# A new order in two mixers and a mask added by a matrix product, in a one-core transformer kernel

## The reference, cut to what matters

```python
# hybrid mixer: x_lru, z, xbc, dt come from one projection h @ w_in
y_lru = rg_lru(causal_conv(x_lru)) * gelu(gate)      # a recurrence over time
xbc = silu(causal_conv(xbc)); xs, bm, cm = split(xbc)
y = ssd_chunked(xs, dt, a, bm, cm) + d * xs           # needs cm @ bm^T per group
out = concat(y_lru, rms_norm(y * silu(z))) @ w_out

# matrix-memory mixer (mlstm): 4 heads of width 512
hh = head_layer_norm(mlstm_chunkwise(q, k, v, i, f))
out = ((hh * norm_g + skip * xc) * silu(z)) @ w_down

# attention kind C: 16 query heads of 64, 2 key heads, a window of 128, a sink per head
sc = where(mask, q @ k^T / 8, -inf)
m = max(max(sc), sink);  p = exp(sc - m)
out = (p / (sum(p) + exp(sink - m))) @ v @ w_out
```

## Time and profile before

| | |
|---|---|
| median of 3 runs | 2538.01 us (2534.19 to 2540.05) |
| profiled execution | 2538.91 us, its span 2537.1 us |
| TensorE (PE) busy | 2421.6 us, 95% |
| VectorE (DVE) busy | 1750.9 us, 69% |
| ScalarE (ACT) busy | 1197.2 us, 47% |
| GpSimd (POOL) busy | 99.5 us, 4% |
| mean granted clock of TensorE | 0.983 |
| instructions | 46504 |

### The profile page before, as it was taken

How to read it: one execution, slowest core, us unless ns; L and a number is a source line. 1 busy time by engine, 2 the same in 40 slices (tenths; PEclk the granted TensorE clock), 3 DMA queues, 4 the chain that set the end, 5 groups by cost and what they waited for, 6 DMA issues and landing times.

```text
span 2537.1 us, 46504 instructions
## 1 busy us (share of the span) xinstructions
PE 2421.6 (95%) x19275; PEld 2325.5 (92%) x19275; DVE 1750.9 (69%) x2240; ACT 1197.2 (47%) x1488; POOL 99.5 (4%) x168
## 2 busy tenths in 40 slices
PE   5999899999999998899998999999998899998998
PEld 5999888999999988899987999889997799987998
DVE  7787788777777865555586755777657666686665
ACT  5334854433433654333455434655335543556433
POOL 2110000010010000000000000110000000000000
PEclk8999999999999999999999999999999999999999
DMA  8886455787687432355433555325552255443552
GB/s 314 318 306 242 154 187 208 252 289 271 239 286 277 160 133 79 118 200 184 152 145 117 182 182 182 133 101 182 183 183 97 84 199 198 150 149 117 190 191 100
DMA packets 75417, 471.49 MB, mean 186 GB/s; under 512 B 8616, under 2 KB 9000, under 8 KB 26664
## 3 DMA queue, kind: packets, MB, share of 16 engines
q1 hardware_dynamic: 56288, 400.79, 43.8%
q0 software_dynamic: 18432, 67.12, 7.5%
q10 hardware_dynamic: 584, 2.00, 0.2%
HBM read 468.83 MB, written 1.05 MB: 185 GB/s over the span
## 4 chain that ended last, share of the span: by engine, by line
PE 81%; DVE 9%; ACT 6%; issue 3%; DMA 1%; SPq 0%; ACTq 0%; DVEq 0%
PE bank L2135 23%; PE bank L2137 23%; PE bank L2136 22%; ACT w_hi L615 2%; PE bank L2146 2%; PE bank L2141 2%; DVE w_lo L1243 2%; PE bank L2142 2%; ACT ARENA L891 1%; DVE ARENA L1432 1%; DVE ARENA L1699 1%; DVE ARENA L1696 1%; PE bank L2213 1%; PE bank L2219 1%; DVE XT L1346 1%
## 5 line engine op out<-in xcount | busy, mean ns | idle before, releaser
L1243 DVE TENSOR_TENSOR w_lo<-w_raw,w_hi 128x2048 fp32r<-128x2048 f32 x369 | 845.6, 2293 | 357.2 <-ACT w_hi L615 356.2
L615 ACT ACTIVATE w_hi<-w_raw 128x2048 fp32r<-128x2048 f32 x371 | 707.9, 1911 | 545.7 <-PE bank L2137 535.1
L2135 PE MATMUL bank<-h_hi,w_hi 128*128 128x256 f32 x3376 | 950.4, 282 | 0.7 <-issue 0.3
L2137 PE MATMUL bank<-h_hi,w_lo 128*128 128x256 f32 x3376 | 941.0, 279 | 0.0
L2136 PE MATMUL bank<-h_lo,w_hi 128*128 128x256 f32 x3376 | 939.9, 278 | 0.0
L2135 PEld LDWEIGHTS bank<-h_hi,w_hi 128*128 128x128 f32 x3376 | 633.3, 188 | 8.4 <-issue 7.8
L2136 PEld LDWEIGHTS bank<-h_lo,w_hi 128*128 128x128 f32 x3376 | 633.7, 188 | 3.6 <-issue 3.3
L2137 PEld LDWEIGHTS bank<-h_hi,w_lo 128*128 128x128 f32 x3376 | 634.2, 188 | 0.0
L2135 PE MATMUL bank<-d_hi,w_hi 128*128 128x256 f32 x1920 | 545.6, 284 | 18.5 <-DVE d_lo L1599 9.2
L2137 PE MATMUL bank<-d_hi,w_lo 128*128 128x256 f32 x1920 | 540.4, 281 | 0.0
L2136 PE MATMUL bank<-d_lo,w_hi 128*128 128x256 f32 x1920 | 540.1, 281 | 0.0
(11 more groups left out here) (383 smaller groups left out, 2355.0 us busy)
## 6 DMA issues: line engine op xcount, KB each, us to landing
w_raw<-in_ws SPq DMA_DIRECT2D x371, 1024.0 KB, 4.8
ada_wbuf<-in_ada POOLq DMA_DIRECT2D x128, 512.0 KB, 5.3
ARENA<-in_first SPq DMA_DIRECT2D x8, 1024.0 KB, 20.0
work<-in_x SPq DMA_DIRECT2D x1, 1024.0 KB, 9.8
ARENA<-in_wax ACTq DMA_DIRECT2D x1, 1024.0 KB, 4.7
out_y<-ARENA SPq DMA_DIRECT2D x4, 256.0 KB, 2.1
ARENA<-in_wg ACTq DMA_DIRECT2D x1, 768.0 KB
c_rows<-in_c SPq DMA_DIRECT2D x1, 512.0 KB, 5.4
```

Of the source, the lines that this page charges most:

```text
L615: act.activation(w_hi[:, slot, :], w_raw[:, slot, :], ACT.Copy).then_inc(hi_ready, 1)
L1243: dve.tensor_tensor(w_lo[:, s, :], w_raw[:, s, :], w_hi[:, s, :].bitcast(F32), ALU.subtract).then_inc(lo_ready, 1)
L2135: pe.matmul(o, whi, xhi, start=start, stop=False, skip_group_check=True)
L2137: return pe.matmul(o, wlo, xhi, start=False, stop=stop, skip_group_check=True)
```

## The change

In the hybrid mixer two steps change places with others: `mix0` goes from behind `cb0` to ahead of `dt2`, and `in11` goes ahead of `cb0`.

In the matrix-memory mixer part 0 is split in step `b` of the last head, ahead of `outputs` of the head before; part 1 at the end of step `c`; and every later part one round of the loop sooner. `outputs` of the last head falls into its three passes, `normed`, `skipped` and `opened`, in rounds 2, 3 and 4 of the loop.

In kind C the mask is no longer added by VectorE. TensorE opens each score bank with a product of the identity and the mask, both in fp32r, and adds the scores to it. VectorE takes the maxima from the bank, a head at a time, and ScalarE takes the exponentials from the bank. The scores of unit u (but for 2) now wait for the exponentials of u-1, where they waited for its maxima. Two copies ahead of the second feed-forward stage make the fp32r operands. Kinds A and B are as before.

```diff
-...dt0 in6 te1 dt1 in7 te2 in8 te3 in9 sqrt dt2 in10 bcs0 xs0 cb0
-   mix0 in11 xs1 xs2 xs3 dt3 scan0 in12 turn0 in13 dec0 ...
+...dt0 in6 te1 dt1 in7 te2 in8 te3 in9 sqrt mix0 dt2 in10 bcs0 xs0
+   in11 cb0 xs1 xs2 xs3 dt3 scan0 in12 turn0 in13 dec0 ...

+        c_mask_r = sb("c_mask_r", [P, 384], F32R)
+        ident_r = sb("ident_r", [P, P], F32R)

 exponentials (ScalarE):
-                        ins = act.activation(pr[:, h, lo_c:hi_c], sc[:, h, lo_c:hi_c], ACT.Exp,
+                        src = score_banks(st, u)[h][:, lo_c:hi_c] if st["key"][0] == "C" else sc[:, h, lo_c:hi_c]
+                        ins = act.activation(pr[:, h, lo_c:hi_c], src, ACT.Exp,

 masked (VectorE):
+                if kind == "C":
+                    for k, (lo_c, hi_c) in enumerate(SEG):
+                        for h in range(2):
+                            link(dve.tensor_reduce(stat[:, 2 * k + h:2 * k + h + 1], score_banks(st, u)[h][:, lo_c:hi_c],
+                                                   AX_X, ALU.max))
+                else:
                     (the additions and the two reductions, as before)

 mlstm (VectorE), where outputs(k) is now normed(k), skipped(k), opened(k):
+                def output_part(c):
+                    dve.wait_ge(m_y, c // 2 + 1)
+                    split_pair(st, c, xm_in[:, 2 * c:2 * c + 2, :], False)
...
                         if k + 1 < MH:
                             block_diagonals(4 * k + 4, 4)
+                        if k == MH - 1:
+                            output_part(0)
                         if k:
                             outputs(k - 1)
...
                         if k == MH - 1:
-                            for c in range(2):
-                                split_pair(st, c, xm_in[:, 2 * c:2 * c + 2, :], False)
+                            output_part(1)
                 for c in range(PARTS["mlstm"]):
-                    if c >= 2:
-                        dve.wait_ge(m_y, c // 2 + 1)
-                        split_pair(st, c, xm_in[:, 2 * c:2 * c + 2, :], False)
+                    if 1 <= c < PARTS["mlstm"] - 1:
+                        output_part(c + 1)
                     lo_ahead(n0 + 16 + c + 2)
-                    if c == 3:
-                        outputs(MH - 1)
+                    if c == 2:
+                        normed(MH - 1)
+                    elif c == 3:
+                        skipped(MH - 1)
+                    elif c == 4:
+                        opened(MH - 1)
                     ada_slot()

 lambda_columns (VectorE, ahead of the second feed-forward stage):
+                dve.tensor_copy(c_mask_r[:, :], c_mask[:, :])
+                link(dve.tensor_copy(ident_r[:, :], ident[:, :]))

 scores (TensorE):
-                    if st["soft"] + u:
+                    if kind == "C" and u != SCORES_MOVE[kind]:
+                        pe.wait_ge(p_ready, st["soft"] + u)
+                    elif st["soft"] + u:
                         pe.wait_ge(negm_ready, st["soft"] + u)
...
+                if kind == "C":
+                    for h in range(2):
+                        pe.matmul(banks[h][:, 0:384], ident_r[:, :], c_mask_r[:, :], start=True, stop=False,
+                                  skip_group_check=True)
...
+                        opens = kind == "A"
-                        pe.matmul(banks[h][:, 0:256], Q[rows, u, P:T], keys, start=True, stop=True)
+                        pe.matmul(banks[h][:, 0:256], Q[rows, u, P:T], keys, start=opens, stop=True, skip_group_check=True)
```

More of the change, by code:

```diff
@@ L102, in mlstm_sequence @@
     return seq
-HYBRID = """in0 in1 in2 lru0 in3 lru1 in4 lru2 in5 lru3 te0 dt0 in6 te1 dt1 in7 te2 in8 te3 in9 sqrt dt2 in10 bcs0 xs0 cb0
-            mix0 in11 xs1 xs2 xs3 dt3 scan0 in12 turn0 in13 dec0 in14 head0 dec1 in15 head1 dec2 in16 head2 dec3 in17 head3
+HYBRID = """in0 in1 in2 lru0 in3 lru1 in4 lru2 in5 lru3 te0 dt0 in6 te1 dt1 in7 te2 in8 te3 in9 sqrt mix0 dt2 in10 bcs0 xs0
+            in11 cb0 xs1 xs2 xs3 dt3 scan0 in12 turn0 in13 dec0 in14 head0 dec1 in15 head1 dec2 in16 head2 dec3 in17 head3
             dec4 row0 mul0 head4 dec5 row1 sum0 head5 dec6 row2 nrm0 head6 dec7 row3 head7 mul1 row4 sum1 nrm1 row5 row6
@@ L1689, in masked @@
                 kind, stat, sc = st["key"][0], stat_of[u % 2], sc_of[u % 2]
-                mask = a_mask if kind == "A" else c_mask
                 dve.wait_ge(s_ready, st["att"] + u + 1)
@@ L1694, in masked @@
                     dve.wait_ge(w_ready, st["soft"] + u - 1)
-                for h in range(2):
-                    link(dve.tensor_tensor(sc[:, h, :], score_banks(st, u)[h][:, 0:384], mask[:, :], ALU.add))
-                chained()
-                for k, (lo_c, hi_c) in enumerate(SEG):
-                    link(dve.tensor_reduce(stat[:, 2 * k:2 * k + 2], sc[:, :, lo_c:hi_c], AX_X, ALU.max))
+                if kind == "C":
[5 more added lines that the diff above has]
+                    for h in range(2):
+                        link(dve.tensor_tensor(sc[:, h, :], score_banks(st, u)[h][:, 0:384], a_mask[:, :], ALU.add))
+                    chained()
+                    for k, (lo_c, hi_c) in enumerate(SEG):
+                        link(dve.tensor_reduce(stat[:, 2 * k:2 * k + 2], sc[:, :, lo_c:hi_c], AX_X, ALU.max))
                 chained()
@@ L1958, in centre, with normed, skipped @@
                     ins.then_inc(m_vc, 1)
-                def outputs(k):
+                marks = [0] * 4
+                def normed(k):
                     dve.wait_ge(m_rs, k + 1)
                     dve.wait_ge(m_hh, 2 * k + 2)
-                    marks = []
-                    for t in range(4 * k, 4 * k + 4):
+                    for i, t in enumerate(range(4 * k, 4 * k + 4)):
                         h = xm_in[:, t, :]
-                        marks.append(link(dve.scalar_tensor_tensor(
+                        marks[i] = link(dve.scalar_tensor_tensor(
                             out=h, in0=h, scalar=col("mlstm_norm_g", t), in1=rstd[:, :],
-                            op0=ALU.mult, op1=ALU.mult)))
+                            op0=ALU.mult, op1=ALU.mult))
+                def skipped(k):
                     for i, t in enumerate(range(4 * k, 4 * k + 4)):
@@ L1974, in outputs, with opened @@
                             op0=ALU.mult, op1=ALU.add))
+                def opened(k):
                     dve.wait_ge(proj_ready, st["evac"] + 8 + (2 * k + 2))
@@ L1982, in outputs @@
                     ins.then_inc(m_y, 1)
+                def outputs(k):
+                    normed(k)
+                    skipped(k)
+                    opened(k)
+                def output_part(c):
+                    dve.wait_ge(m_y, c // 2 + 1)
+                    split_pair(st, c, xm_in[:, 2 * c:2 * c + 2, :], False)
                 for step, k in mlstm_sequence():
@@ L2339, in scores @@
                         keys = K[rows, u, :] if kind == "A" else KD[rows, u // 4, :]
-                        pe.matmul(banks[h][:, 0:256], Q[rows, u, P:T], keys, start=True, stop=True)
-                        last = pe.matmul(banks[h][:, 256:384], Q[rows, u, 0:P], keys[:, 0:P], start=True, stop=True)
+                        opens = kind == "A"
+                        pe.matmul(banks[h][:, 0:256], Q[rows, u, P:T], keys, start=opens, stop=True, skip_group_check=True)
+                        last = pe.matmul(banks[h][:, 256:384], Q[rows, u, 0:P], keys[:, 0:P], start=opens, stop=True,
+                                         skip_group_check=True)
                 last.then_inc(s_ready, 1)
```

## The result

| | before | after |
|---|---|---|
| runs of the first comparison | 2538.01, 2540.05, 2534.19, 2545.75 us | 2520.81, 2505.95, 2500.34, 2513.08 us |
| median | 2539.03 us | 2509.51 us |
| ratio, 95% interval | | 0.9873 [0.9847, 0.9900] |
| profiled execution, span | 2538.91, 2537.1 us | 2520.81, 2519.0 us |

The kernel is faster, as forecast. The median, 2509.51 us, lies inside the range of 2507 to 2524. The two profiles differ by only 18.1 us.

What follows compares the result with a forecast made beforehand. TensorE sets the pace at its upper clock, so only its waits could be won: hybrid 7.2, matrix memory 14.8 and kind C 2.5 make 24.5; 2538.9 less that is 2514.4, less 0.9 to the median 2513.5 us, range 2507 to 2524.

Steps and rivals of the forecast that it cites:

- less 1 for the runs' spread: Range of the whole time: 1 us allowed for run spread below the low end of 2508, likewise above 2523.
- the tightest place: Hybrid mixer: in12, reader of the delayed low half of piece 12, with 0.3 us of slack.
- The filled gap alone, 5.6: Hybrid mixer, lower bound of the gain: in11 fills 5.6 of the 7.3 us TensorE waits before cb0.
- Rival D: Hybrid mixer: the gap only moves, dec0 still waits on another late VectorE link; gain 2, time 2518.5 us; chance 0.06.
- the low clock, 2.8 + 2.6: Matrix-memory mixer: slow clock behind the 4.39 us gap (2.8) and the 4.52 us gap (2.6) goes too.
- Rival B: Matrix-memory mixer keeps one gap, a late high half delaying a part; 4.5 + 2.6 stay, 2520.5 us; chance 0.09.
- The serial loop: Kind C: scores, maxima and exponentials become serial, 5.0 us a unit, under today's 6.1.
- The relief there: Kind C, stretch bound by VectorE (S2 to S5): four units save 0.85 us each, 3.4.
- the price of the added wait: Kind C: 0.9 us taken off the gain, for scores at 1.2 GHz in a serial loop.
- the 3 us named as a sign of failure: Kind C: scores waiting over 3 us for line 891 would show the forecast wrong.
- A: Kind C loses: waiting for exponentials outweighs the saved additions as waits halve the clock; -3, time 2519 us; chance 0.09.
- C: Kind C: scores also wait behind ScalarE's transposed weights and outputs, 9.7 us a unit against 6.1; 2541 us; chance 0.03.

Runs made afterwards that it cites:

- c_wait: The kernel before, with only kind C's scores made to wait for the exponentials of the unit before instead of its maxima; 2545.06 us in its run.

## Why the prediction was right or wrong

**Direction and sum: right, the sum in part by luck.** Forecast 24.5 us, at one cadence about 25; the parts are off by +1.0, -1.7 and +1.4 us, which nearly cancel. The ratio stands for 32.2 us: some 7 of them are the draw and not the change.

| part | forecast | stage lengths (profiles) | gain |
|---|---|---|---|
| hybrid | 7.2 | 160.5 (8), 152.3 (10) | 8.2 |
| matrix memory | 14.8 | 228.0 (8), 214.9 (10) | 13.1 |
| kind C | 2.5 | 89.2 (9), 85.3 (9) | 3.9 |

**The step that failed** is in the range: "less 1 for the runs' spread" and "1 for the spread", and with it the silent premise that a stretch with a granted clock of 1.00 takes the same time in every execution, so that the three runs shown (2534 to 2540) spanned it. In all 83 runs of the kernel before it took 2524.9 to 2555.2 us, mean 2539.5; even the median of a set of 7 to 25 runs went from 2534.8 to 2548.3. The forecast itself named 5 us as what a measurement can tell, and the range did not use it. With 5 us for the draw in place of 1 it would have been 2503 to 2528 and held 2505.8. The miss of 1.2 us is itself far smaller than the draw: by the medians of the same eight runs the time was inside.

**Hybrid.** The working was right to 0.1 us: cb0 to the first decay product 7.25 against 7.2, VectorE last, in12 the tightest place (0.45 us late, where 0.3 of slack was expected). "The filled gap alone, 5.6" was no lower bound: the filled gap alone gives 0.27. The stage gained 8.2 on the mean: 7.1 from cb0 to the first decay product, 0.7 behind it, where the clock fell in four of eight profiles with the old order and in one of ten with the new, and 0.4 ahead of cb0, where nothing was changed. Rival D didn't come.

**Matrix memory.** Every wait named went, in the place and size named. In the two profiles compared the stretch from the last head's scores to the sum of squares went from 75.70 to 61.15 us, 14.55 against the forecast 14.8. The term mis-sized against typical executions is the low clock, 2.8 + 2.6: that stretch is 74.1 to 74.8 us in the other profiles, so that they have 1.3 us less of it. Rival B didn't come.

**Kind C.** The serial loop was named rightly, but the 2.5 us were all to come between unit 0 and unit 7, which was to be 38 to 41 us long. It is 41.8 on the mean of nine changed profiles (40.5 to 42.4; after itself 41.78), 42.62 to 42.65 without the change: 0.8 us. The relief there was sized well, 45.0 in c_wait less 41.8, thus 3.2 against 3.4; the term mis-sized is the price of the added wait, 2.4 us where 0.9 was taken. The other 3.0 us of the stage's 3.9 lie behind unit 7, for which the forecast had no term: there the last unit's maxima and exponentials stand in the open, and with the shorter wait (2.35 us for 3.84) the clock no longer falls. That the stage as a whole gained more than forecast is luck of that. Three units wait (2.33, 0.78, 1.79 us), short of the 3 us named as a sign of failure. The four reductions are 1.15 us from the bank against 1.2 forecast, the exponential 460 ns against 493 from SBUF. The trace doesn't agree: 419 ns for one head's 256 columns from the bank stand beside 407 for 256 elements from SBUF in the earlier trace rows, 12 ns more. Rivals A and C didn't come; c_wait gives the loss that A feared, 3.3 us, and the relief outweighed it.

## What to carry to other kernels

Where two engines are bound within a few us of each other, move both or neither: one edit alone gave 0.3 and 1.5 us, both 7.25. Compare stretch by stretch on several executions and count the products in windows of equal length; a clock of 1.00 doesn't say that two executions run alike, and a difference of 1% can be decided only by stages or when the draw is settled, here with 12 cheap products. A wait's price is its length plus a low clock that sometimes follows and sometimes not; a range needs both. And a sum that comes out right says little of its parts: check each gain in the place where it was forecast.

## What the runs showed of the hardware

- Back-to-back fp32r products of 128 x 128 weights and 256 moving columns start 113 or 118 ns apart at a granted clock of 1.00. Most stages keep one of the two; in the last four it was drawn anew in each execution (113 ns in 24 of 40 stages of ten profiles). One fp32 product in each body had it at 118 ns in all 40 stretches of one profile, 12 products with 16 columns of weights had it at 113 ns in all 16 of the last stages in four profiles, 12 with 128 columns did not settle it. No run shows why, nor why the second and third stage could not be switched.
- Behind one and the same wait, 1.4 to 2.2 us long, the granted clock fell in four of eight executions and stayed at 1.00 in the others, the longest wait among these. Other waits were followed by it every time, as the 7.3 us at cb0 and the 4.5 us among the row pieces. Behind unit 7 of kind C it fell after each of ten waits of 3.83 to 4.69 us and after none of ten of 2.02 to 2.37.
